# A mixture-of-experts kernel: expert outputs go back to tokens by a pure one-hot in two fp32r passes, with the gate applied earlier

## What is computed

```python
def moe_ffn(xf, w_router, b_router, w_up, b_up, w_down, b_down):
    logits = (xf @ w_router + b_router).astype(jnp.float32)
    top_vals, top_idx = lax.top_k(logits, TOP_K)
    gates = jax.nn.softmax(top_vals, axis=-1)
    ...
        h = xb @ w_up[e] + b_up[e]
        glu = jnp.minimum(h[:, :D_EXPERT], SWIGLU_LIMIT)
        lin = jnp.clip(h[:, D_EXPERT:], -SWIGLU_LIMIT, SWIGLU_LIMIT)
        act = glu * jax.nn.sigmoid(SWIGLU_ALPHA * glu) * (lin + 1)
        return act @ w_down[e] + b_down[e]
    ...
    contrib = y_pad[dest].astype(jnp.float32) * gates.reshape(-1)[order][:, None]
    return jnp.zeros((T, D), jnp.float32).at[sorted_tok].add(contrib).astype(xf.dtype)
...
    f = moe_ffn(v.reshape(Bn * T, D), w_router, b_router, w_up, b_up, w_down, b_down)
    y = layer_norm(DEEPNORM_ALPHA * h + gate2 * f.reshape(Bn, T, D), ln2_g, ln2_b)
```

## Time and profile before

| what | before |
|---|---|
| median of 3 runs | 1458.26 us (two at 1457.79 and 1458.26, one disturbed at 7709.62) |
| span of the profiled execution | 1457.4 us |
| PE busy | 1342.7 us (92%) |
| DVE busy | 465.8 us (32%) |
| ACT busy | 259.6 us (18%) |
| POOL busy | 143.9 us (10%) |
| DMA, mean over the span | 320 GB/s, 466.32 MB |
| chain that ended last | PE 84%, DVE 6%, DMA 5% |

### The profile page before, as it was taken

One profiled execution on the slowest core, in us unless ns is written; L12 is line 12 of the kernel. 1 busy time (PEld: TensorE's weight loads), 2 busy tenths in 40 slices (PEclk: granted clock), 3 DMA queues, 4 the chain that ended last, 5 costly groups with the idle time before them and its releaser, 6 DMA issues.

```text
span 1457.4 us, 17200 instructions
## 1 busy us (share of the span) xinstructions
PE 1342.7 (92%) x6107; PEld 553.5 (38%) x6108; DVE 465.8 (32%) x885; ACT 259.6 (18%) x412; POOL 143.9 (10%) x86
## 2 busy tenths in 40 slices
PE   4699999769999999999999999999999999999991
PEld 0499954423333333333333333333333333333330
DVE  1706745742222222222222222222222222222236
ACT  0333200201111111121211111121111111111212
POOL 0557362040000000000000000000000000000003
PEclk9599999779999999999999999999999999999996
DMA  9634598849999999999939999992999999299941
GB/s 325 206 116 176 190 366 297 319 149 361 393 393 395 396 396 393 393 393 393 394 125 361 393 393 393 394 396 107 360 393 393 393 395 396 104 363 393 393 172 36
DMA packets 186804, 466.32 MB, mean 320 GB/s; under 512 B 6491, under 2 KB 6523, under 8 KB 183425
## 3 DMA queue, kind: packets, MB, share of 16 engines
q1 hardware_dynamic: 184913, 460.23, 84.6%
q0 software_dynamic: 1872, 5.84, 1.2%
HBM read 464.19 MB, written 1.85 MB: 320 GB/s over the span
## 4 chain that ended last, share of the span: by engine, by line
PE 84%; DVE 6%; DMA 5%; ACT 2%; issue 1%; SPq 1%; DVEq 0%; POOL 0%; ACTq 0%
PE bank L786 34%; PE bank L814 17%; PE bank L757 9%; PE bank L581 8%; PE bank L701 7%; DMA ring<-in_w_ada 2%; PE bank L760 2%; DMA hx<-in_x_sample 2%; PE bank L804 2%; ACT front L918 1%; PE bank L710 1%; PE bank L798 1%; PE bank L776 1%; DMA mod_rows<-tail_rows 1%; DVE u_low L991 1%
## 5 line engine op out<-in xcount | busy, mean ns | idle before, releaser
L786 PE MATMUL bank<-ring,front 128*64 128x512 f32 x2240 | 510.1, 597 | 0.0
L1202 DVE TENSOR_TENSOR front<-front,bank 128x512 f32<-128x512 f32 x175 | 120.4, 688 | 539.2 <-PE bank L757 534.9
L786 PEld LDWEIGHTS bank<-ring,front 128*64 128x64 f32 x2240 | 155.5, 137 | 309.8 <-issue 304.7
L814 PE MATMUL bank<-ring,front 128*64 128x512 f32 x1120 | 248.0, 595 | 26.7 <-ACT front L918 26.7
L757 PE MATMUL bank<-front 128*128 128x512 f32 x288 | 143.0, 619 | 2.6 <-ACT front L921 1.5
L814 PEld LDWEIGHTS bank<-ring,front 128*64 128x64 f32 x1120 | 79.9, 137 | 172.4 <-issue 172.4
L910 ACT ACTIVATE front<-front 128x256 f32<-128x256 f32 x70 | 29.2, 417 | 577.2 <-DVE front L1219 577.2
L505 POOL TENSOR_TENSOR front<-front,tail_rows 128x1024 f32<-128x1024 f32 x2 | 4.8, 2409 | 1120.6 <-ACT front L874 1120.6
L701 PE MATMUL bank<-front 128*64 128x512 f32 (+1 forms) x432 | 106.5, 611 | 0.0
L1219 DVE TENSOR_SCALAR front<-bank 128x256 f32<-128x256 f32 x70 | 29.7, 424 | 206.0 <-PE bank L786 206.0
L581 PE MATMUL bank<-u_high,ring_parts 128*128 128x320 f32 x512 | 80.8, 316 | 9.5 <-ACT u_high L834 5.7
(11 more groups left out here) (206 smaller groups left out, 814.8 us busy)
## 6 DMA issues: line engine op xcount, KB each, us to landing
ring<-in_w_up SPq DMA_DIRECT2D x256, 1024.0 KB, 9.9
ring<-in_w_down SPq DMA_DIRECT2D x64, 2048.0 KB, 10.0
ring<-in_w_ada SPq DMA_DIRECT2D x12, 2048.0 KB, 16.2
ring<-in_w_in SPq DMA_DIRECT2D x8, 2048.0 KB, 12.5
ring<-in_w_o SPq DMA_DIRECT2D x2, 2048.0 KB, 19.2
hx<-in_x_prompt SPq DMA_DIRECT2D x2, 1024.0 KB, 23.7
ring<-in_w_out_a SPq DMA_DIRECT2D x1, 2048.0 KB, 7.8
ring<-in_w_out_b SPq DMA_DIRECT2D x1, 2048.0 KB, 16.5
```

What stands on the lines that cost most here:

```text
L786: last = mm(bank[b][64 * h:64 * h + 64, :], x_T[:, k % 4, 64 * (k // 4):64 * (k // 4) + 64], w[:, :, h * 256:(h + 1) * 256], start=False, ...
L814: last = mm(bank[B_DOWN][64 * h:64 * h + 64, :], act_T[:, q, 64 * hh:64 * hh + 64], ring[:, s, (k % 4) * 1024 + h * 512:(k % 4) * 1024 + ( ...
L1202: signal(TT(Y[:, i, :], Y[:, i, :], bank[b][:, :], ALU.add), bank_free[b], value)
```

## The change

- `gated`, `S_gate`, `P_gate`, `O_rows` and their transposes go. The gate is applied to the activation: `slot_gate`, one number per slot, is the third factor of the activation on VectorE.
- `token_rows` is new: two bf16 matmuls per round give, in every row, the rank and the gate of each token for the present expert, from `route_parts` (rank and gate of all tokens by expert, as three bf16 parts each). VectorE compares the ranks with the slot numbers (`onehot_T`, a 0/1 matrix with the slots twice, in rows 0 to 63 and 64 to 127) and sums gate times one-hot along the row to `slot_gate`.
- The down result is split: ScalarE copies it to `O_high` as fp32r, VectorE writes the rest to `O_low`. `combine(n, t)` is four fp32r matmuls of 64 rows: high and low, each for the two halves h, which stand in rows 0 to 63 and 64 to 127. The calls are spread: t=0 inside j=0, t=1 behind j=0, t=2 inside j=1.
- `gather` moves from behind j=0 to behind both up projections. The transposes of `act_rows` go ahead of those of the next rows. The loop's transposes of the activated rows no longer wait for a copy of `P_gate`.
- The down bias is no longer the first `combine`: six fp32 matmuls ahead of the loop give `gates @ b_down`, and ScalarE writes them to `Y`. `Y` has six pieces (the 64 new tokens lie in rows 0 to 63 of two of them), so the moves of half a piece at the end go, and so does the clearing of `Y`.
- Ahead of the loop are new: rank and gate written three times side by side, their transposes, two copies by ScalarE, and eight VectorE steps that make `route_parts`. TensorE waits for these (`route_ready`) before the loop.
- In the loop VectorE ends with `O_low`, which waits for `O_high`. The constants grow by 257 columns.

The diff, cut to its core:

```diff
-        S_gate = region(front, 6664, 3, P)
...
+        route_parts = region(front, 7632, NT).bitcast(BF16)
+        weighed = region(front, 7952, NT)
+        b_down_rows = region(front, 12392, 2, 512)
+        route_T = region(front, 13416, 2, NT)
+        Y = region(front, 14180, 6, 512)
+        route_rows = region(front, 17934, 2, 3, 3 * E)
+
+
+        onehot_T = nc.alloc_sbuf_tensor_at("onehot_T", [P, 3 * P], F32R, offset=start + 4 * (RING * CH + 6664))
+        O_high = nc.alloc_sbuf_tensor_at("O_high", [P, 512], F32R, offset=start + 4 * (RING * CH + 11368))
+        O_low = nc.alloc_sbuf_tensor_at("O_low", [P, 512], F32R, offset=start + 4 * (RING * CH + 11880))
...
-            pool.memset(O_rows, 0.0).then_inc(O_cleared, 1)
-            pool.wait_ge(O_cleared, 1)
-            pool.dma_start(O_rows[0:E, :, :], a["b_down"][0].rearrange("e (h m) -> e h m", h=2)).then_inc(b_down_landed, 16)
+            pool.dma_start(b_down_rows[0:E, :, :], a["b_down"][0].rearrange("e (h m) -> e h m", h=2)).then_inc(b_down_landed, 16)
+            pool.memset(onehot_T[:, :].bitcast(F32), 0.0).then_inc(onehot_ready, 1)
+            pool.memset(O_high[:, :].bitcast(F32), 0.0).then_inc(O_high_ready, 1)
+            pool.memset(O_low[:, :].bitcast(F32), 0.0).then_inc(O_low_ready, 1)
...
+            def route_transposes(name, i):
+                ps = take(name)
+                for t in range(3):
+                    r = ROWS[t]
+                    last = nc.tensor.transpose(ps[0:3 * E, t * P:t * P + r], route_rows[0:r, i, t, :], ident[0:r, 0:r])
+                done(name, last)
+
+            def bias(pieces):
+
+                for i in pieces:
+                    t, h = divmod(i, 2)
+                    ps = take(f"bias{i}")
+                    done(f"bias{i}", mm(ps[0:ROWS[t], :], route_T[0:E, 1, t * P:t * P + ROWS[t]], b_down_rows[0:E, h, :],
+                                        start=True, stop=True))
+
+            pe.wait_ge(softmax_ready, 1)
+            route_transposes("gate_T", 1)
+            wait_read(pe, "gate_T")
+            pe.wait_ge(b_down_landed, 16)
+            bias((0, 1, 2))
             pe.wait_ge(rounds_ready, 1)
             ps = take("bounds")
             done("bounds", mm(ps[0:E, 0:1], tri_incl[0:E, :], rounds[0:E, :], start=True, stop=True))
+            bias((3, 4, 5))
             pe.wait_ge(passed_ready, 1)
             ps = take("table")
             mm(ps[0:1, 0:NROUND], ones[0:E, 0:1], passed[0:E, :], start=True, stop=True)
             mm(ps[0:1, NROUND:2 * NROUND], rounds[0:E, :], passed[0:E, :], start=True, stop=True)
             done("table", mm(ps[0:1, 2 * NROUND:2 * NROUND + E], rounds[0:E, :], tri_incl[0:E, :], start=True, stop=True))
-
-            wait_read(pe, FRONT[[n for n in range(len(FRONT)) if n % 8 == B_X][-1]])
+            route_transposes("rank_T", 0)
...
-            def combine(n, pieces):
-
-                for i in pieces:
-                    b = COMBINE_BANKS[i]
-                    if i == 0:
-                        pe.wait_ge(O_ready, 2 * n + 2)
-                        pe.wait_ge(Pg_ready, n + 1)
-
-                    pe.wait_ge(bank_free[b], front_uses(b) + PER_ROUND[b] * n + COMBINE_BANKS[:i].count(b))
-                    if i < 4:
-                        t, h = divmod(i, 2)
-                        last = mm(bank[b][:, :], P_gate[:, t * P:(t + 1) * P], O_rows[:, h, :], start=True, stop=True)
-                    else:
-                        for h in range(2):
-                            last = mm(bank[b][64 * h:64 * h + 64, :], P_gate[:, 2 * P:NT], O_rows[:, h, :],
-                                      start=True, stop=True)
-                    last.then_inc(bank_full[b], 1)
+
+            def token_rows(n):
+
+                for i, b in ((0, B_T), (1, B_XT)):
+                    mm(bank[b][:, 0:NT], up_sel[0:3 * E, :], route_parts.rearrange("p (i t) -> p i t", i=2)[0:3 * E, i, :],
+                       start=True, stop=True).then_inc(bank_full[b], 1)
+
+            def combine(n, t):
+
+                if t == 0:
+                    pe.wait_ge(onehot_ready, n + 1)
+                    pe.wait_ge(O_high_ready, n + 1)
+                    pe.wait_ge(O_low_ready, n + 1)
+                for h in range(2):
+                    b = B_C[h]
+                    pe.wait_ge(bank_free[b], front_uses(b) + PER_ROUND[b] * n + t)
+                for part, stop in ((O_high, False), (O_low, True)):
+                    for h in range(2):
+                        rows = slice(64 * h, 64 * h + 64)
+                        last = mm(bank[B_C[h]][:, :], onehot_T[rows, t * P:(t + 1) * P], part[rows, :], start=not stop, stop=stop)
+                        if stop:
+                            last.then_inc(bank_full[B_C[h]], 1)
 
             pe.wait_ge(table_ready, 1)
             G = pe.value_load(table[0:1, 159:160], min_val=1, max_val=52)
             pe.wait_ge(b_up_ready, 1)
+            for b in (B_T, B_DOWN):
+                wait_read(pe, FRONT[[n for n in range(len(FRONT)) if n % 8 == b][-1]])
+            pe.wait_ge(route_ready, 1)
...
-                            combine(g, (2 * j, 2 * j + 1))
+                            combine(g, 2 * j)
+                            if j == 1:
+                                token_rows(g)
                     last.then_inc(bank_full[b], 1)
                     if j == 0:
-                        gather(g + 1, x_rows_read=g + 1)
-                combine(g, (4,))
-                pe.wait_ge(gate_ready, g + 1)
-                for t in range(3):
-                    r = ROWS[t]
-                    last = nc.tensor.transpose(bank[B_T][:, t * P:t * P + r], S_gate[0:r, t, :], ident[0:r, 0:r])
-                last.then_inc(bank_full[B_T], 1)
-                x_transposes(g + 1, xT_read=g + 1)
+                        combine(g, 1)
+                gather(g + 1, x_rows_read=g + 1)
                 pe.wait_ge(act_ready, 2 * g + 2)
-                pe.wait_ge(Pg_ready, g + 2)
                 for q in range(4):
                     last = nc.tensor.transpose(bank[B_T][:, q * P:(q + 1) * P], act_rows[:, q * P:(q + 1) * P], ident)
                 last.then_inc(bank_full[B_T], 1)
+                x_transposes(g + 1, xT_read=g + 1)
                 pe.wait_ge(actT_ready, g + 1)
                 for k in range(KC):
                     s = expert_slot(4 + k // 4)
@@ -816,7 +846,8 @@
                     if k == 3:
                         last.then_inc(chunk_used[s], 1)
                 last.then_inc(bank_full[B_DOWN], 1)
-            combine(G, range(5))
+            for t in range(3):
+                combine(G, t)
...
+            def route_copy(name, i):
+                ps = wait_full(act, name)
+                free(name, AF(route_T[0:3 * E, i, :], ps[0:3 * E, 0:NT], ACT.Copy))
+
+            route_copy("gate_T", 1)
+            for i in range(6):
+                ps = wait_full(act, f"bias{i}")
+                r = ROWS[i // 2]
+                free(f"bias{i}", AF(Y[0:r, i, :], ps[0:r, :], ACT.Copy))
+            route_copy("rank_T", 0)
             x_copy(0)
             xT_copy(0)
             act.wait_ge(table_ready, 1)
@@ -908,22 +949,15 @@
                 for j in range(2):
                     act.wait_ge(glu_ready, 2 * g + j + 1)
                     AF(sig[:, j, :], glu[:, j, :], ACT.Sigmoid, scale=SWISH).then_inc(sig_ready, 1)
-                    if j == 0:
-                        x_copy(g + 1)
-
-                act.wait_ge(bank_full[B_T], front_uses(B_T) + 2 * g + 1)
-                AF(P_gate[0:SLOTS, :], bank[B_T][0:SLOTS, 0:NT], ACT.Copy).then_inc(Pg_ready, 1)
-                xT_copy(g + 1)
+                x_copy(g + 1)
                 act.wait_ge(bank_full[B_T], front_uses(B_T) + 2 * g + 2)
                 AF(act_T[:, :, :], bank[B_T][:, :].rearrange("p (q s) -> p q s", q=4), ACT.Copy).then_inc(actT_ready, 1)
+                xT_copy(g + 1)
                 act.wait_ge(bank_full[B_DOWN], g + front_uses(B_DOWN) + 1)
-                for h in range(2):
-                    AF(O_rows[0:SLOTS, h, :], bank[B_DOWN][64 * h:64 * h + 64, :], ACT.Copy).then_inc(O_ready, 1)
+                AF(O_high[:, :], bank[B_DOWN][:, :], ACT.Copy).then_inc(O_high_ready, 1)
...
-                signal(v.tensor_copy(up_sel, sel3[:, bass.ds(e, 1)].to_broadcast([P, SLOTS])), sel_ready, n + 1)
-
-            def gated(n, e):
-
-                signal(TT(S_gate[:, :, 0:SLOTS], S, by_slot(gate[:, :, bass.ds(e, 1)]), ALU.mult), gate_ready, n + 1)
-
+                signal(v.tensor_copy(up_sel, sel3[:, bass.ds(e, 1)].to_broadcast([P, P])), sel_ready, n + 1)
...
+            step(v.tensor_copy(copies(0), each_copy(rank)))
...
+            step(v.memset(route_parts, 0.0))
+
+            wait_read(dve, "gate_T")
+            wait_read(dve, "rank_T")
+            parts = route_parts.rearrange("p (i t) -> p i t", i=2)
+            step(v.tensor_copy(parts[0:3 * E, :, :], route_T[0:3 * E, :, :]))
+            for q in (1, 2):
```

(53 more changed lines are left out.)

74 lines of the change are left out of this document (25 added, 49 removed).

## The result

| what | before | after |
|---|---|---|
| median | 1458.03 us (4 runs, one disturbed at 7709.62) | 1399.28 us (4 runs, 1397.48 to 1401.58) |
| ratio to before | | 0.9607, 95% interval 0.9594 to 0.962 |
| span of the profiled execution | 1457.4 us | 1399.8 us |
| PE busy | 1342.7 us (92%) | 1259.7 us (90%) |
| DVE busy | 465.8 us (32%) | 540.1 us (39%) |

Forecast were 1394 us (1378 to 1414). The kernel became 3.9% faster. TensorE's own round shrank by 3.54 us, which in 35 rounds would be 124 us; 59 us arrived.

What follows compares the result with a forecast made beforehand. The prediction took TensorE to pace the kernel, with DMA taking over after the change. Start 321.3 plus loop 1031.8 plus end 39.7 gave a span of 1392.8 us, so a median of 1394, range 1378 to 1414.

Steps and rivals of the forecast that it cites:

- What bounds: In the loop: TensorE paces before, DMA hard behind; no round averages under 31.92 us between pauses.
- TensorE's round: TensorE's work per loop round falls from 31.66 to 28.1 us with row halves side by side, 29.4 if not.
- The loop: First chunk issue in the loop to last down projection: 1031.8 us, DMA-paced except a near tie in the last stretch.
- Ahead of the loop: Start of the loop 3.4 us later: more constants 0.35 us, making route_parts 3 us.
- run while VectorE works on the ranks: Ahead of the loop: six bias matmuls and nine transposes are covered; uncovered they would add up to 7 us.
- The copies that make `route_parts`: VectorE ahead of the loop, held up by GpSimd: 3 us taken, bounds 0.5 and 7.
- Behind the loop: End 4.5 us later: V behind O_low costs 7.0, third tile wins 2.5; 39.7 us after the last down projection.
- The moved gather: In the round: its 2.89 us cost nothing by itself, covering the clamps and activation of j=1.
- DMA did not have room: Rival for the loop: DMA can exceed 394 GB/s, at 419 giving 1349 us; chance 0.07.
- the clock did not fall: Rival in the loop: chunk waits lower TensorE's clock, each fall about 2 us, time near 1474; chance 0.06.
- Fp32r on half the rows: Rival in combine: it costs what fp32 costs, 0.86 us per matmul, round 37.0 us, time 1653; chance 0.03.
- the time to landing: Sign in the loop: it grows to many chunks, 20 us and more, since SyncE issues far ahead.

Runs made afterwards that it cites:

- light_after: Kernel after, with the second down chunk of each expert in the loop loading 1 MiB in place of 2: 1347.07 us, ratio 0.9246.
- light_before: Kernel before, with the second down chunk of each expert in the loop loading 1 MiB in place of 2: 1456.31 us, ratio 0.9988.
- dose_after: Kernel after, with both passes of every combine made twice: 1406.85 us, ratio 0.9659.
- pool_late: Kernel after, with GpSimd's nine operations on hx waiting until route_parts is done: 1396.03 us, ratio 0.9588.
- bias_late: Kernel after, with the last two of the six bias matmuls moved behind the gather of the first rows: 1395.30 us, ratio 0.9568.
- early_start: Kernel after, with VectorE's first bias selection ahead of route_parts and the wait for route_ready moved to the first token rows: 1392.58 us, ratio 0.9576.
- all_three: Kernel after, with early bias selection, O_low behind V at the end and late bias matmuls: 1386.89 us, ratio 0.9511.
- all_four: Kernel after, with early bias selection, O_low behind V, late bias matmuls and GpSimd's hx work behind route_parts: 1383.81 us, ratio 0.9501.
- early_v: Kernel after, with O_low made at the head of the next round, and behind V after the loop: 1390.21 us, ratio 0.9554.
- gather_back: Kernel after, with the gather moved back behind j=0: 1437.0 us, ratio 0.9862.

## Why the prediction was right, point by point

The sum was made on the span: 1392.8 against 1399.8.

**What bounds: right.** The price of a round was read off a transfer that nobody waited for: 31.92 us, measured 31.93. The loads run at 394 GB/s in both kernels. `light_after` and `light_before` show the bound move, `dose_after` shows that TensorE's time is free where DMA sets the pace.

**TensorE's round: right to 0.1 us** (28.1, measured 28.12). The row halves do run side by side (`dose_after`), the nearer of the two bounds.

**The loop: 1031.8 forecast, 1033.4 measured.** Each stretch is within 1.0 us. Even the near tie of the last one held: `dose_after` shows that TensorE decides it.

**Ahead of the loop: mis-sized.** From the last v transposes to the first matmul I forecast 3 more, measured are 6.1 (30.4 to 36.5). The table's first matmul divides this span. First the kernel before, then the kernel after:

```profile
300.57 0.37 PE L731 MATMUL bank<-front,const 32*1 32x64 f32 x2 [6.18 <-DVE front L1175]
```

```profile
302.98 5.67 PE L748 MATMUL bank<-front 32*128 32x512 f32 x6
...
303.13 2.33 POOL L504 TENSOR_TENSOR hx<-hx,front 64x1024 f32<-64x1024 f32 x1
...
303.33 2.17 DVE L1206 TENSOR_SCALAR front<-const,front 32x64 f32<-32x64 f32 x1
...
308.58 0.37 PE L762 MATMUL bank<-front,const 32*1 32x64 f32 x2
...
309.38 0.21 DVE L1209 TENSOR_SCALAR table<-bank 1x64 int32<-1x64 f32 x1 [3.48 <-PE bank L764]
```

It starts 19.4 us behind the transposes before and 24.5 after, 5.1 later; from there to the loop it is 11.1 and 12.0, 1.0 more. The step that failed is that the bias matmuls "run while VectorE works on the ranks", a term taken at nothing. VectorE has its part ready (L1206) 21.4 us behind the transposes, 2.1 later than L1175 before, but TensorE still works on the last three bias matmuls (L748, at a granted clock of 0.50) and starts the table 3.1 us later; VectorE waits 3.48 us for it. With VectorE undisturbed, in `pool_late`, the table comes just as late. The copies that make `route_parts`, the term that I did work out at 3 us, stand behind the table, where 1.0 us more came (2.3 against the second profile of the front before). That the total lies between my bounds of 0.5 and 7 is no credit to the working. Each cause hides the other: `pool_late` gives 2.5 us back, `bias_late` 0.6, `early_start`, which takes `route_parts` out of the way, 3.7; with the bias matmuls and `route_parts` both out of the way, in `all_three` and `all_four`, the loop starts over 7 us earlier. TensorE's clock came up 0.5 us earlier in the first round. The other 2.5 us of the profile's miss lie ahead of the transposes, where repeated profiles scatter by 7 us; 132 KB more of constants shifts TensorE's first matmul by 0.4 us (5.96 to 6.35), as forecast.

**Behind the loop: right.** 40.0 us after the last down projection, forecast 39.7. L1299 starts 10.0 us behind it (9.6 forecast). In the third tile the slow pair of 4.71 us became 0.68 and 1.28:

```profile
1385.32 0.68 DVE L1299 TENSOR_TENSOR front<-bank,tail_rows 64x512 f32<-64x512 f32 x1
1386.04 1.28 DVE L1302 TENSOR_TENSOR front<-front 64x512 f32<-64x512 f32 x1
```

That is 2.75 us won, 2.5 forecast. `early_v` shows what the order cost.

**The moved gather: right.** That it now covers the clamps and the activation of j=1 is what `gather_back` shows, and what it is worth: 38 us, of which some 12 are the falls of the clock that the uncovered wait brings.

**The rivals.** DMA did not have room: no slice of the loop is above 396 GB/s. By the Trainium skill (DMA: Bandwidth & Descriptors, Bandwidth) 425 GB/s were to be had; the loop's rows show 394. In the kernel after the clock did not fall: 1.00 in every round of the loop, with waits of up to 1.1 us, so what the Trainium skill's TensorE: Matmul & The Clock Gate (HAM oscillation) warns of did not happen at waits of this length. At a wait of 2.04 us it did happen, in ten rounds of `gather_back`, for 1.25 us each and not the 2 us that the prediction takes. It is the new place of the gather that keeps such a wait out of the round. Fp32r on half the rows kept its price: 0.23 us a pair. That row tiles multiply in parallel (the Trainium skill's TensorEngine Tiling (Array Packing), Key Properties) is what `dose_after` shows.

**A sign that was wrong.** I forecast that the time to landing would grow to 20 us and more. It stops at a median of 14.7, because SyncE itself is held; see the last section. The pause of DMA at a repeat did shrink as forecast, from 24.6 to 11.1 us (forecast some 25 to about 10).

## What to carry to other kernels

Before counting what an engine will save, ask how much faster the next one in line can go, and read it from its backlog: a time to landing that grows from round to round by 0.26 us told the new bound of 31.92 us while no wait in the trace pointed to it. A stretch in which the second resource stands still (here DMA in each repeated round) is what a saving on the first can still buy, no more. And when a wait goes to the end of a loop's body, look at what used to run beside the last round: 8 us here came out from under a down projection, and a reordering brought them back. Ahead of a loop, where two engines take turns, look for both of them before calling a term covered: each move alone gave 0.6 and 2.5 us here.
